# Scan preparation with four PSUM areas and compact norms, window keys loaded from another queue, exponentials scaled on POOL

## The reference, cut to what matters

```
# RWKV-7 branch, per token and head (8 heads of 64)
w_log = -softplus(-(w0 + tanh(w_lo) @ w_decay_up)) - 0.5
decay = exp(-exp(w_log))
a  = sigmoid(a0 + a_lo @ w_iclr_up);   g = sigmoid(g_lo) @ w_gate_up
kk = k * k_k;   kk = kk / max(sqrt(sum_head(kk * kk)), 1e-12)
k  = k * (1 + (a - 1) * k_a)
y, state = scan(r, decay, k, v, -kk, kk * a)
# attention branch, per query head: compressed, selected and window part
p = softmax(q . k / 8, masked);   o = sum of gate * (p @ v) over the three parts
# merge gates of the two branches: sigmoid(h @ w_gates), 2 x 1024 columns
```

## Time and profile before

| what | value |
|---|---|
| median of three runs | 1644.14 us (1641.23 to 1644.26) |
| profiled execution, whole | 1645.93 us |
| its span, first to last instruction | 1644.3 us |
| PE, PEld, DVE, ACT, POOL busy | 78%, 49%, 31%, 16%, 11% of the span |
| mean granted PE clock | 0.879 |

### The profile page before, as it was taken

One profiled execution on the slowest core, in us unless ns is written; L12 is line 12 of the kernel. 1 busy time (PEld: TensorE's weight loads), 2 busy tenths in 40 slices (PEclk: granted clock), 3 DMA queues, 4 the chain that ended last, 5 costly groups with the idle time before them and its releaser, 6 DMA issues. The chain is left out here.

```text
span 1644.3 us, 26410 instructions
## 1 busy us (share of the span) xinstructions
PE 1279.5 (78%) x10642; PEld 798.6 (49%) x10642; DVE 510.9 (31%) x1011; ACT 266.5 (16%) x540; POOL 186.4 (11%) x247
## 2 busy tenths in 40 slices
PE   5999959989994586688334899929878878887881
PEld 4875545779993454445223785523333323333330
DVE  2002364845646352654332211251111101110113
ACT  2000232401220122443000001201111101110110
POOL 0000250200000430111311000001101111111000
PEclk9999977899998697799666999959989989998996
DMA  7021121151001853332534661159999999999974
GB/s 302 16 81 63 46 68 59 67 132 18 5 4 57 245 180 108 99 102 104 163 122 177 223 273 64 42 192 336 406 406 405 414 405 411 407 413 406 415 296 169
DMA packets 85482, 324.84 MB, mean 198 GB/s; under 512 B 25249, under 2 KB 53074, under 8 KB 70682
## 3 DMA queue, kind: packets, MB, share of 16 engines
q1 hardware_dynamic: 69578, 293.86, 46.9%
q0 software_dynamic: 11184, 25.17, 4.7%
q10 hardware_dynamic: 4608, 4.20, 0.8%
HBM read 306.32 MB, written 28.92 MB: 204 GB/s over the span
## 5 line engine op out<-in xcount | busy, mean ns | idle before, releaser
L2465 DVE TENSOR_TENSOR e_g<-e_g,PS 64x512 f32<-64x512 f32 x32 | 22.1, 690 | 333.1 <-ACT e_g L2432 333.1
L281 PE MATMUL PS<-scr,p_w 128*128 128x272 f32 (+2 forms) x448 | 105.7, 399 | 6.1 <-DVE scr L348 6.1
L884 PE MATMUL PS<-scr 128*128 128x272 f32 x384 | 92.2, 404 | 21.1 <-DMA scr<-in_w_gates 21.1
L2378 PE MATMUL PS<-first,e_xs 128*64 128x512 f32 x352 | 88.2, 659 | 22.8 <-DMA first<-in_w_exp_up 22.1
L2378 PE MATMUL PS<-second,e_xs 128*64 128x512 f32 x352 | 86.8, 650 | 24.5 <-DMA second<-in_w_exp_up 23.8
L2378 PE MATMUL PS<-e_w,e_xs 128*64 128x512 f32 x320 | 80.3, 660 | 23.5 <-DMA e_w<-in_w_exp_up 23.5
L281 PEld LDWEIGHTS PS<-scr,p_w 128*128 128x128 f32 (+2 forms) x448 | 84.0, 188 | 27.4 <-issue 6.9
L884 PEld LDWEIGHTS PS<-scr 128*128 128x128 f32 x384 | 75.1, 196 | 37.7 <-DMA scr<-in_w_gates 21.8
L2036 PE MATMUL PS<-m_oT,xe 128*128 128x272 f32 x256 | 64.7, 413 | 22.4 <-DMA m_oT<-scratch_ob_dram 17.8
L2321 POOL DMA_INDIRECT xe<-scratch_h_dram,toks x32 | 30.5, 954 | 387.7 <-PE PS L2368 276.8
L293 PE MATMUL PS<-p_w,scr 128*128 128x512 f32 (+1 forms) x192 | 70.7, 529 | 0.0
(11 more groups left out here) (535 smaller groups left out, 2038.7 us busy)
## 6 DMA issues: line engine op xcount, KB each, us to landing
first<-in_w_exp_gate SPq DMA_DIRECT2D x11, 2048.0 KB, 18.0
first<-in_w_exp_up SPq DMA_DIRECT2D x11, 2048.0 KB, 22.4
first<-in_w_exp_down SPq DMA_DIRECT2D x11, 2048.0 KB, 23.3
second<-in_w_exp_gate SPq DMA_DIRECT2D x11, 2048.0 KB, 27.3
second<-in_w_exp_up SPq DMA_DIRECT2D x11, 2048.0 KB, 31.7
second<-in_w_exp_down SPq DMA_DIRECT2D x11, 2048.0 KB, 22.9
e_w<-in_w_exp_gate SPq DMA_DIRECT2D x10, 2048.0 KB, 27.5
e_w<-in_w_exp_up SPq DMA_DIRECT2D x10, 2048.0 KB
```

The lines of the kernel that those rows point to most:

```text
L281: last = nc.tensor.matmul(out[:, n], w[:, s % NW, c, a:a + m], hT[:, c, n * TH:n * TH + TH], start=(c == 0), stop=(c == KC - 1))
L884: last = M(gate_ps(u)[:, n], wgate[:, u % 2, c, :], hT[:, c, n * TH:n * TH + TH], start=(c == 0), stop=(c == KC - 1))
L2378: last = M(ps, xs[:, b, c, :], w[s][m][:, c * DE:c * DE + DE], start=(c == 0), stop=(c == KC - 1))
L2465: V.tensor_tensor(g[:, b, :], g[:, b, :], psU, ALU.mult).then_inc(h_out, 1)
```

## The change

Four things are changed together.

- `rwkv`, PSUM: `wide` has four areas in place of two (the two further ones are those of the gates). The LoRA products rotate through four; products 2 and 3 wait until gates 2 and 3 are out, and from product 4 on each waits for the output of the one four before it.
- `rwkv`, norms: the four head sums now go into one area of 8 rows (one per head, `headsum`), are clipped, rooted and inverted as 8 x 544, and are spread to the 128 rows of each c by four products with `headrow`, which has 8 rows; DVE multiplies from PSUM. Gates 4 and 5 stand between the sums and the spreading, gates 6 to 11 behind it. DVE clips the norms ahead of the scans, and updates k ahead of the multiplication (through `BK` in place of `a_`).
- The first two slices of the gate weights are loaded at the end of the input projection's list, and the gates 0 and 1 wait for nothing.
- Prompt attention: POOL multiplies `E` itself by the coefficient (2 n elements per row, in place), and PE turns the blocks by plain transposes against the unit matrix. Sample attention: ACT issues the load of the second half's window keys when the first half's selected scores are done, into the places of those pages' keys.

```diff
-            return PS[:, (k % 2) * 1024:(k % 2) * 1024 + T]
+            return PS[:, (k % 4) * 1024:(k % 4) * 1024 + T]
...
+                for u in range(2):
+                    sp.dma_start(wgate[:, u], io["w_gates"][u, 0]).then_inc(wgate_in, 16)
                 sp.wait_ge(h_stored, 16)
+                sp.wait_ge(wgate_in, 32)
...
+                dve.wait_ge(kk_mm, 1)
+                link(V.tensor_scalar(kka[0:8, 0, 0:T], wide(0)[0:8], 1e-24, None, ALU.max))
+                dve.sem_inc(root_in, 1)
                 dve.wait_ge(v_mixed, 1)
                 dve.wait_ge(lora_out, 12)
...
                 dve.sem_inc(scanned, 1)
+                dve.wait_ge(root_out, 1)
+                link(V.reciprocal(kka[0:8, 0, 0:T], kka[0:8, 0, 0:T]))
+                dve.sem_inc(norm_ready, 1)
                 for c in range(4):
-                    dve.wait_ge(kk_mm, c + 1)
-                    link(V.tensor_scalar(kka[:, c, 0:T], wide(c), 1e-24, None, ALU.max))
-                    dve.sem_inc(root_in, 1)
-                dve.sem_inc(kk_used, 1)
+                    link(V.tensor_scalar(BK[:, c, 1, 0:T], a_[:, c, 0:T], 1.0, Pm("k_a", c), ALU.subtract, ALU.mult))
+                    link(V.scalar_tensor_tensor(out=k_[:, c, 0:T], in0=BK[:, c, 1, 0:T], scalar=1.0, in1=k_[:, c, 0:T],
+                                                op0=ALU.add, op1=ALU.mult))
                 for c in range(4):
-                    dve.wait_ge(root_out, c + 1)
-                    link(V.reciprocal(kka[:, c, 0:T], kka[:, c, 0:T]))
-                    link(V.tensor_tensor(kk[:, c, 0:T], kk[:, c, 0:T], kka[:, c, 0:T], ALU.mult))
+                    dve.wait_ge(norm_mm, c + 1)
+                    link(V.tensor_tensor(kk[:, c, 0:T], kk[:, c, 0:T], wide(c % 2), ALU.mult))
+                    dve.sem_inc(kk_used, 1)
...
                         u = 3 * c + j
-                        if u >= 2:
-                            pe.wait_ge(lora_out, u - 1)
+                        if u in (2, 3):
+                            pe.wait_ge(gate_out, u + 1)
+                        if u >= 4:
+                            pe.wait_ge(lora_out, u - 3)
                         mmT(u, P, lhsT, rhs).then_inc(lora_mm, 1)
+                pe.wait_ge(lora_out, 9)
                 for c in range(4):
                     pe.wait_ge(kk2_ready, c + 1)
-                    pe.wait_ge(lora_out, min(11 + c, 12))
+                    for ts in (slice(0, 512), slice(512, T)):
+                        last = M(wide(0)[0:8, ts], cst["headsum"][:, 8 * c:8 * c + 8], kka[:, c, ts], start=(c == 0), stop=(c == 3))
+                last.then_inc(kk_mm, 1)
+                pe.wait_ge(lora_out, 12)
+                for u in (4, 5):
+                    gates(u)
+                pe.wait_ge(hrow_in, 16)
+                pe.wait_ge(norm_ready, 1)
+                for c in range(4):
                     if c >= 2:
-                        pe.wait_ge(root_in, c - 1)
-                    mmT(c, P, cst["blockones"], kka[:, c, 0:T]).then_inc(kk_mm, 1)
-                for u in range(4, NGATE):
+                        pe.wait_ge(kk_used, c - 1)
+                    mmT(c % 2, P, hrow[:, c * P:c * P + P], kka[0:8, 0, 0:T]).then_inc(norm_mm, 1)
+                for u in range(6, NGATE):
                     gates(u)
...
-                            last = M(psP(g)[:, j * P:j * P + P], E[:, k % 3, g, j * P:j * P + P], diag[:, k % 3, g],
-                                     start=True, stop=True)
+                            last = X(psP(g)[:, j * P:j * P + P], E[:, k % 3, g, j * P:j * P + P], cst["ident"])
...
-                    nc.gpsimd.tensor_tensor(diag[:, k % 3], cst["ident"].unsqueeze(1).to_broadcast([P, 2, P]),
-                                            co[:, k % 3, :].unsqueeze(2).to_broadcast([P, 2, P]), ALU.mult
-                                            ).then_inc(diag_ready, 1)
+                    e = E[:, k % 3, :, 0:n]
+                    nc.gpsimd.tensor_tensor(e, e, co[:, k % 3, :].unsqueeze(2).to_broadcast([P, 2, n]), ALU.mult
+                                            ).then_inc(scaled, 1)
...
-                sp.wait_ge(o_mm, 1)
-                for b in range(4):
-                    sp.dma_start(wkv[:, b], io["win_kv"][4 + b]).then_inc(win_in, 16)
...
+                    if hf == 0:
+                        act.wait_ge(sel_mm, 1)
+                        for b in range(4):
+                            act.dma_start(late_win[:, b].rearrange("p (c k) n -> p c k n", k=2), io["win_kv"][4 + b]).then_inc(win_in, 16)
```

More of the change, by code:

```diff
@@ L50, in shape_constants @@
     c["blockones"] = (p[:, None] // HD == p[None, :] // HD)
+    c["headsum"] = np.concatenate([2 * i + p[:, None] // HD == np.arange(8)[None, :] for i in range(4)], 1)
     c["ones"] = np.ones((P, P))
@@ L91, in shape_constants @@
     c["iota_c"] = np.repeat(np.arange(CAP)[None, :], P, 0)
+    c["headrow"] = np.concatenate([p[:, None] == 2 * i + p[None, :] // HD for i in range(4)], 1)
     out, at, cols = {}, 0, []
@@ L101 @@
 CONST_AT, CONSTS = shape_constants()
+NCST = CONST_AT["headrow"][0]
 PAR_AT = {}
@@ L416, in rwkv @@
         wup = t("r_wup", [64, 512])
+        hrow = t("r_hrow", [8, 512])
+        hrow_in = sem("r_hrow_in")
         wgu = t("r_wgu", [96, 512])
@@ L541, in _ @@
                 sp.dma_start(shift[:], io["shift_in"]).then_inc(par_in, 16)
+                sp.dma_start(hrow[:], io["consts"][0:8, NCST:NCST + 512]).then_inc(hrow_in, 16)
                 sp.wait_ge(last_rows, 1)
                 sp.dma_start(io["shift_out"], lastz[:]).then_inc(shift_dma, 16)
-                for u in range(2):
-                    sp.dma_start(wgate[:, u], io["w_gates"][u % 2, u // 2]).then_inc(wgate_in[u], 16)
                 for u in range(NGATE):
@@ L819, in _ @@
                     A(g_[:, c, 0:T], wide(3 * c + 2), ACT.Copy).then_inc(lora_out, 1)
-                for c in range(4):
-                    act.wait_ge(root_in, c + 1)
-                    A(kka[:, c, 0:T], kka[:, c, 0:T], ACT.Sqrt).then_inc(root_out, 1)
+                act.wait_ge(root_in, 1)
+                A(kka[0:8, 0, 0:T], kka[0:8, 0, 0:T], ACT.Sqrt).then_inc(root_out, 1)
                 gate_value(4)
@@ L1602, in _ @@
                 for k in range(N):
+                    n = P * (units[k][0] + 1)
                     pool.wait_ge(co_ready, k + 1)
-                    if k >= 3:
-                        pool.wait_ge(turn_mm[1], k - 2)
-                    nc.gpsimd.tensor_tensor(diag[:, k % 3], cst["ident"].unsqueeze(1).to_broadcast([P, 2, P]),
-                                            co[:, k % 3, :].unsqueeze(2).to_broadcast([P, 2, P]), ALU.mult
-                                            ).then_inc(diag_ready, 1)
+                    e = E[:, k % 3, :, 0:n]
+                    nc.gpsimd.tensor_tensor(e, e, co[:, k % 3, :].unsqueeze(2).to_broadcast([P, 2, n]), ALU.mult
+                                            ).then_inc(scaled, 1)
             @block.scalar
@@ L1670, in sample_attention @@
         kvs = (kv_first, t("s_kv", [P, 4, NPAGES, 2, PAGE]))
+        late_win = kv_first[:, :, 0:8, 0, :]
         qrow = t("s_qrow", [TSM, 512])
@@ L1740, in _, with window @@
                     kv = kvs[hf]
+                    def window(b, c, k):
+                        return late_win[:, b, 2 * c + k] if hf else wkv[:, b, c, k]
                     if hf:
@@ L1750, in _ @@
                     for b, r, q in tiles:
-                        last = M(PS[r, WINB:WINB + 512], q, wkv[:, b, :, 0, :], start=True, stop=True)
+                        last = M(PS[r, WINB:WINB + 512], q, late_win[:, b, 0:8:2] if hf else wkv[:, b, :, 0, :], start=True, stop=True)
                     last.then_inc(small_mm, 1)
@@ L1793, in _ @@
                         for b, r, q in tiles:
-                            M(PS[r, OB + P:OB + 2 * P], pT[:, 16 + c, r], wkv[:, b, c, 1, :], start=(c == 0), stop=False)
+                            M(PS[r, OB + P:OB + 2 * P], pT[:, 16 + c, r], window(b, c, 1), start=(c == 0), stop=False)
                     for b, r, q in tiles:
```

30 lines of the change are left out of this document (14 added, 16 removed).

## The result

The changed kernel takes 1614.5 us (median of four runs, 1612.5 to 1620.4) against 1642.8 of the kernel before (four runs): ratio 0.983, 95% interval 0.9815 to 0.985. That is some 28 us faster. The forecast was 10 faster, 1634, with a range of 1612 to 1649: the sign was right, the time lies in the range, and the size is wrong by almost a factor of three.

What follows compares the result with a forecast made beforehand. Each stage had its own limit: PE in preparation, a hand-off loop including PE in prompt attention, a chain of waits in sample attention. -13 - 10 + 13 = -10: 1636 us profiled, 1634 median, range 1612 to 1649.

Steps and rivals of the forecast that it cites:

- with half the turning gone, the first three tiles have PE idle more than in that stretch almost everywhere: Prompt attention: PE idles more than at 698.8 to 702.2 (busy 2.44 of 3.40 us), after which the clock was 0.50.
- three tiles mostly slow and the last, which is dense, fast: Prompt attention: 6.4 + 8.4 + 3 - 2.8 = +15, less about 2 paid before: +13 us.
- At an undisturbed clock the sum gave -8: Prompt attention at full clock: turn starts 0.2 later, is 0.98 shorter; -0.8 per last-tile pair, -8 us in all.
- the one rule weighed: Prompt attention: skill's rule on transposes would make the last tile slow too; the forecast held trace rows against it.
- Forecast 13 to 14: Preparation: earlier gate weights, LoRA in four areas, compact norms; -13 to -14 us, taken as -13.
- the third slice's wait: Preparation: third gate-weight slice loads only after ACT empties the first gate; 0.6 us charged, bounds 0 and 1.3.
- third product: Preparation: third norm-broadcast product on PE waits until DVE has used the first; taken as 290, 285 to 291.5.
- the clock through LoRA hangs on the waits: Preparation: four areas remove the wait, LoRA 19.3 to 8.8 us at 2.4 GHz; rival LoRA slow, 1645, chance 0.22.
- DVE and POOL do meet: Preparation: DVE's k update takes turns with POOL's subtractions; preparation -13 us, or -20 if they don't meet.
- moves as a whole: Chunk scan behind the preparation: shifts with it, no term of its own in the sum.
- -10 taken: Sample attention: ACT loads the second half's window keys earlier, then SP's last page is late; -8 to -10.4 us.
- attention keeps its clock: Rival, prompt attention: clock stays up, -8 us there, -31 in all, 1613; chance 0.20.

Runs made afterwards that it cites:

- window keys alone: Kernel before with only ACT's load of the second half's window keys: 1636.1 us, ratio 0.9951.
- preparation alone: Kernel before with only the preparation's part (gate weights a stage earlier, four areas, compact norms): 1629.2 us, ratio 0.9918.
- turned by matmuls, scaled: Changed kernel with blocks turned by matmuls against the identity in place of transposes, POOL still scaling: 1622.5 us, ratio 0.9867.
- scaling alone: Kernel before with only the prompt attention's part (exponentials scaled on POOL, turned by transposes): 1638.6 us, ratio 0.9981.
- changed, second profile: The changed kernel run once more without edits, against the kernel before: 1613.4 us, ratio 0.9827.
- changed, k update moved, second profile: Changed kernel with DVE's k update moved ahead of the head sums, run again beside the fill runs: 1609.4 us, ratio 0.9782.
- changed, two areas: Changed kernel with LoRA back in two PSUM areas, all else kept: 1628.6 us, ratio 0.9898.
- changed, k update moved, first profile: Changed kernel with DVE's eight k update instructions moved ahead of the head sums, first run: 1613.0 us, ratio 0.9803.
- changed, fills: Changed kernel with two 512-column zero-weight matmuls ahead of each attention turn from the ninth unit on: 1613.3 us, ratio 0.9806.
- changed, fewer fills, k update moved: Changed kernel, k update moved, one zero-weight matmul per turn from the ninth unit through the third tile, two in the last: 1610.4 us, ratio 0.979.
- changed, fills in the last tile, k update moved: Changed kernel, k update moved, two zero-weight matmuls per turn in the last attention tile only: 1606.9 us, ratio 0.9772.

## Why the prediction was right and wrong, point by point

The attention in all profiled runs: its time, its mean granted clock, its last tile (from the third output taken out to the fourth), the time at 1.2 GHz behind its slow start (the first 24 to 28 us), and the unit, of 32, at which POOL was when such a fall began. Each tile has eight units; units 25 to 32 are the last tile's:

| kernel | attention us | clock | last tile us | us at 1.2 GHz | falls at unit |
|---|---|---|---|---|---|
| before | 131.8 | 0.90 | 24.2 | 3.4 | 14 |
| window keys alone | 131.6 | 0.90 | 25.7 | 3.4 | 32 |
| preparation alone | 128.2 | 0.94 | 24.2 | 0 | none |
| turned by matmuls, scaled | 131.7 | 0.91 | 24.9 | 0 | none |
| scaling alone | 123.9 | 0.88 | 24.2 | 6.9 | 28, 31 |
| changed, second profile | 123.8 | 0.88 | 24.3 | 6.9 | 28, 32 |
| changed, k update moved, second profile | 126.8 | 0.85 | 27.2 | 13.8 | 28, 32 |
| changed, first profile | 129.4 | 0.84 | 27.1 | 17.0 | 9, 27, 31 |
| changed, two areas | 130.4 | 0.84 | 27.1 | 20.4 | 8, 17, 27, 32 |
| changed, k update moved, first profile | 130.4 | 0.82 | 27.1 | 23.9 | 8, 17, 27, 31 |
| changed, fills | 125.3 | 0.91 | 22.0 | 0 | none |
| changed, fewer fills, k update moved | 126.4 | 0.90 | 22.0 | 0 | none |
| changed, fills in the last tile, k update moved | 122.2 | 0.91 | 22.0 | 0 | none |

**What failed: the share of the attention at 1.2 GHz, and where it lies.** The step is "with half the turning gone, the first three tiles have PE idle more than in that stretch almost everywhere", hence "three tiles mostly slow and the last, which is dense, fast": +13, where the two profiles of the changed kernel measured -2.4 and -8.0. The forecast needed most of the 76 us from the first scores to the last tile (659 to 735 in the trace before) at 1.2 GHz. Behind the slow start, which every kernel has (17 to 25 us), the six profiles that turn by transposes without fills have 7 to 24 us. The error lies in taking one stretch that was followed by a fall as the bound for all: the changed kernel's second and third tile hold stretches with PE busy 1.72 to 1.98 of 3.40 us and keep 2.4 GHz. The row that spoke for it, 2.14 of 3.40 at 1.00, was in the list and got a chance of 0.2. And it came out the other way round by tiles: the second and third tile got faster (25.1 to 22.8 us and 31.8 to 29.0, from the preparation alone to the second profile), while the last, which the forecast exempted, has two falls in each of the six profiles and took 24.2 to 27.2 us where the old form took 24.2. There POOL's scaling is longest, 1.89 us, and the two falls come with PE's waits of 1.95 and 3.01 us for it.

**What held of it: the sizes.** At an undisturbed clock the sum gave -8, of which -7.6 in the last three tiles. Between the preparation alone and the fills in the last tile, both without a fall, these tiles took 25.1 to 22.8, 31.8 to 29.6 and 24.2 to 22.0 us: -6.7. That the scaling alone and the second profile lie 7.9 and 8.0 us under the profile before is partly luck, since the clock fell twice in them and the profile before had a fall and a longer slow start than the preparation alone. (Small slips in the sum: four times 0.8 is 3.2 for the last tile, not 2.8, the four tiles make 8.6, and 1.13 and 1.04 make 2.2; each is worth about 1 us or less.) From 123.8 us at 0.88 to 130.4 at 0.82 the stage loses 6.6 us for 17 us more at 1.2 GHz. So the clock costs about 0.4 us per us, and in the worst profile it takes back most of the gain.

On the one rule weighed: the Trainium skill, "TensorE: Matmul & The Clock Gate", Part 4, says that transposes don't count as busy PE for the clock in the same way. The runs agree in direction: turning by matmuls, the clock fell once for 3.4 us or not at all behind the first 26 us (four profiles), and by transposes two to four times in all six profiles without fills. They don't show that transposes count for nothing, since they also take half the time. The Trainium skill, "TensorE: Matmul & The Clock Gate", Part 1, says that the chip's watch over activity runs free of the kernel, so that the slow stretch varies from run to run; the two profiles of the changed kernel agree for the second tile (a fall in one of them) and the length of the last fall (10.2 and 3.5 us), not for the place of the falls in the last tile, which recur.

**Preparation: right.** Forecast 13 to 14, measured 14.0 by stage, 14 as a kernel. Forecast and measured, in order: gates begin 223.1 / 222.2; the third slice's wait 0.6 / 1.93, beyond the bound of 1.3; LoRA 8.8 / 9.6, PE's own bound, since PE and not ACT set it; scans' end 276.2 / 276.9; norms' reciprocal 279.8 / 280.6; third product 290 / 290.5; gate 6 at 294.5 / 294.9; last gate 341.3 / 340.6. Some of these errors cancel: LoRA ended 1.1 us later than forecast, and from gate 6 to the last gate it took 45.8 us in place of 46.8. Two steps in it were disputed, and runs decided both: the clock through LoRA hangs on the waits (two areas: 19.4 us), and DVE and POOL do meet (the k update moved: gate 6 at 288.0).

**Scan: not in the forecast.** It "moves as a whole" held in the run of the preparation alone and in the second profile (172.8 and 173.0 us); in the first profile of the changed kernel it was 176.3 at 0.92.

**Sample attention: right.** -10 taken; -10.9 by stage, 7 to 9 as a part alone. The order of what is late next was as said: no wait for keys, then 3.98 us for the last pages. On ACT the four issues took 5.63 us, three times the 1.77 priced from SP; that cost nothing here, since ACT then waited for DVE until 797.79.

**The number.** With the second profile's attention the sum would have been -13 - 10 - 8 = -31, the rival "attention keeps its clock", 1613, against 1614.5 measured. It had 0.20. Its number is near, but its condition didn't hold: in none of the six profiles did the clock stay up behind the start.

**What stays open.** Why the clock fell about the start of the second or third tile in three of the six profiles and not in the others, and why the last fall lasted from 3.4 to 10.3 us. Only one execution of each kernel shows its stages, and for several kernels it is the slowest, so how the unprofiled runs were spread is told by their times alone.

## What to carry to other kernels

Price the clock as a range from the profile's own two levels, and let the rows where PE was light and the clock stayed up weigh as much as the one after which it fell. When a light stage stands at that edge, single runs differ by several us, so several executions belong to the verdict, and several profiles show which falls recur: here the two that come with PE's longest waits did. A short wait ahead of a stretch of products can cost far more than itself: four areas in place of two took away a wait of under a microsecond and made that stretch 9.7 us shorter. The length of a wait alone doesn't tell: the 1.93 us ahead of gate 2 let nothing fall. When a new wait is put in, look for work of the engine it waits for that can go into an older wait of that engine: moving eight DVE instructions made the preparation another 4 to 6 us shorter in four profiles.

## What the runs showed of the hardware that was not expected

- Two products of 32 rows each, with weights in partitions 0 to 31 and 32 to 63, ran side by side: at 255.91 and 255.93 one for each of two LoRA outputs started 0.02 us apart, and the four records of 512 columns of the two took 0.97 us together, as long as two such records by 96 rows (0.96 us, from 257.12).
- Products by a weight of zeros held the clock: 1.00 over the 99.3 us with fills.
- Of eight DVE instructions the first two took 1.40 and 1.46 us beside POOL's subtractions, where the same took 0.50 and 0.72 without POOL at work.
- POOL's multiplication with a broadcast operand took 1.67 ns per further element in the new place too (1.892 us for 1024, 1.039 for 512). The Trainium skill, "GPSIMD Engine Reference", section 3.1, led to an estimate of 2.2 us for 1024; the measurement decides.
